# A two-layer decoder trunk: the closing block's seven products reordered with their sums on VectorE, two early weight loads, and one gate step put later

## What is computed

```
even: x + [conv(C*x)*B*silu(g), pooling(u)*silu(g)] @ w_out        after rmsnorm(x) @ w_in
odd:  x + [window attention * silu(g), mLSTM * sigmoid(o) * silu(g)] @ w_out   after rmsnorm(x) @ w_in
out:  rmsnorm(x, final_norm)
```

## Time and profile before

| | |
|---|---|
| median of 3 runs | 1678.21 us (1676.13 to 1678.56) |
| profiled execution, own time | 1675.21 us |
| its span, first to last instruction | 1673.4 us |
| PE busy | 98% of the span |
| granted TensorE clock, mean | 0.996 of full |

### The profile page before, as it was taken

How to read it: one execution, slowest core, us unless ns; L and a number is a source line. 1 busy time by engine, 2 the same in 40 slices (tenths; PEclk the granted TensorE clock), 3 DMA queues, 4 the chain that set the end, 5 groups by cost and what they waited for, 6 DMA issues and landing times.

```text
span 1673.4 us, 20976 instructions
## 1 busy us (share of the span) xinstructions
PE 1643.1 (98%) x7944; PEld 1365.5 (82%) x7944; DVE 869.0 (52%) x1450; ACT 510.2 (30%) x1191; POOL 490.8 (29%) x580
## 2 busy tenths in 40 slices
PE   8999999999999999999999999999999999999996
PEld 8887788888788788888888878888878888888885
DVE  2745335685534662566443475357573236445755
ACT  2000233562200133366310022437441001244732
POOL 8777674547556010000034601000042000100014
PEclk9999999999999999999999999999999999999998
DMA  8887688658898786544679877644498657654456
GB/s 273 312 290 262 221 287 254 207 175 289 302 328 300 260 321 203 168 133 139 239 279 326 290 278 294 199 144 136 143 361 292 196 190 289 241 180 148 138 185 268
DMA packets 180292, 399.18 MB, mean 239 GB/s; under 512 B 34240, under 2 KB 85952, under 8 KB 180192
## 3 DMA queue, kind: packets, MB, share of 16 engines
q1 hardware_dynamic: 157504, 370.20, 64.1%
q10 hardware_dynamic: 22688, 27.64, 5.1%
HBM read 303.35 MB, written 94.44 MB: 238 GB/s over the span
## 4 chain that ended last, share of the span: by engine, by line
PE 89%; DMA 4%; DVE 3%; POOL 2%; issue 1%; ACT 1%; ACTq 0%; POOLq 0%; SPq 0%; DVEq 0%
PE bank L682 14%; PE bank L684 14%; PE bank L683 14%; PE pair_a L682 4%; PE pair_a L684 4%; PE pair_a L683 4%; PE pair_b L682 4%; PE pair_b L684 4%; PE pair_b L683 4%; PE pair_c L682 4%; PE pair_c L684 4%; PE pair_c L683 4%; DMA slot<-split_weights 2%; PE pair_a L1060 2%; PE pair_c L1043 2%
## 5 line engine op out<-in xcount | busy, mean ns | idle before, releaser
L682 PE MATMUL bank<-h_hi,slot 128*128 128x512 f32 (+1 forms) x976 | 381.2, 391 | 2.3 <-DMA slot<-split_weights 1.3
L684 PE MATMUL bank<-h_hi,slot 128*128 128x512 f32 (+1 forms) x976 | 377.4, 387 | 0.0
L683 PE MATMUL bank<-h_lo,slot 128*128 128x512 f32 (+1 forms) x976 | 377.1, 386 | 0.0
L682 PEld LDWEIGHTS bank<-h_hi,slot 128*128 128x128 f32 x976 | 183.8, 188 | 40.5 <-issue 2.7
L684 PEld LDWEIGHTS bank<-h_hi,slot 128*128 128x128 f32 x976 | 183.6, 188 | 37.6
L683 PEld LDWEIGHTS bank<-h_lo,slot 128*128 128x128 f32 x976 | 183.7, 188 | 37.2 <-issue 1.0
L563 POOL TENSOR_TENSOR slot<-stages,slot 128x512 fp32r<-128x512 f32 x132 | 184.9, 1400 | 11.0
L534 POOL TENSOR_TENSOR rs<-sums,eps 128x1 f32<-128x1 f32 x48 | 13.2, 275 | 456.7 <-ACT junk L1197 456.7
L561 POOL TENSOR_SCALAR slot<-stages 128x512 fp32r<-128x512 f32 x132 | 90.6, 686 | 115.1 <-issue 98.3
L624 POOL TENSOR_TENSOR proj<-proj,xin 128x1024 f32<-128x1024 f32 x2 | 4.9, 2444 | 373.6 <-DVE proj L1955 373.6
L682 PE MATMUL pair_a<-h_hi,slot 128*128 128x512 f32 x256 | 101.4, 396 | 1.7 <-DMA slot<-split_weights 1.7
(11 more groups left out here) (349 smaller groups left out, 3428.1 us busy)
## 6 DMA issues: line engine op xcount, KB each, us to landing
slot<-split_weights SPq DMA_DIRECT2D x376, 512.0 KB, 4.4
split_weights<-slot SPq DMA_DIRECT2D x132, 512.0 KB, 4.4
slot<-combined_weights SPq DMA_DIRECT2D x80, 512.0 KB, 5.1
combined_weights<-keys SPq DMA_DIRECT2D x32, 512.0 KB, 5.0
stages<-in_even_w_in SPq DMA_DIRECT2D x48, 256.0 KB, 4.0
stages<-in_odd_w_in SPq DMA_DIRECT2D x36, 256.0 KB, 3.4
stages<-in_even_w_out SPq DMA_DIRECT2D x32, 256.0 KB, 4.0
result<-res ACTq DMA_DIRECT2D x16, 512.0 KB, 7.4
```

Of the source, the lines that this page charges most:

```text
L682: t.matmul(dst, l_hi, r_hi, start=start, stop=False)
L683: t.matmul(dst, l_hi, r_lo, start=False, stop=False)
L684: return t.matmul(dst, l_lo, r_hi, start=False, stop=stop)
```

## The change

1. Only block 3: order Q4, Q1, Q6, Q7, Q5, Q2, Q3 in place of Q2, Q4, Q1, Q5, Q6, Q7, Q3, in other PSUM banks. The four sums and all additions to `res` are DVE's (`last_stage`); POOL keeps the roots. The last tile is scaled and stored in two halves, one by SP and one by ACT. Its tiles 2 and 3 are complete after the fifth product.
2. Loads 0 and 1 of block 1 go to slots 4 and 5, unused in block 0, and are issued before the save of half 128. The ring is turned by four places (`place`).
3. In blocks 1 and 2 the raw loads move from step 0 to step 5, the combined saves from 8 to 35 to 13 to 40.
4. The product `full` and its split move from `gate` of an odd u to `gate` of u + 1, one round later, in all blocks.

```
+ODD_ORDER = ((), (), (Q2, Q4, Q1, Q5, Q6, Q7, Q3), (Q4, Q1, Q6, Q7, Q5, Q2, Q3))
...
+LAST_SUMS = (ODD_SUM2, ODD_SUM3, ODD_SUM1, ODD_SUM4)
...
             def load_half(i):
-                sp.dma_start(slots[i % SLOTS][:, :].bitcast(F32), later[i]).then_inc(s_slot[i % SLOTS], 16)
+                sl = (i + SLOTS0) % SLOTS
+                sp.dma_start(slots[sl][:, :].bitcast(F32), later[i]).then_inc(s_slot[sl], 16)
...
+                if i == HALVES - SLOTS0:
+                    for j in range(SLOTS - SLOTS0):
+                        sp.wait_ge(s_saved[j], 16)
+                        load_half(j)
...
+                sp.wait_ge(s_saved[(SLOTS - SLOTS0 + i) % SLOTS0], 16)
+                sp.wait_ge(s_half, HALVES - SLOTS0 + i + 1)
+                load_half(SLOTS - SLOTS0 + i)
...
-                        if i == 0:
+                        if i == 5:
                             for place in range(4):
                                 load_raw(b - 1, place, 0)
-                        if 8 <= i < 40 and i % 8 < 4:
-                            save_combined(b - 1, 4 * (i // 8 - 1) + i % 8)
+                        if 13 <= i < 41 and (i - 13) % 8 < 4:
+                            save_combined(b - 1, 4 * ((i - 13) // 8) + (i - 13) % 8)
                         if i == 46:
...
+            sp.wait_ge(s_norm, NB * 4)
+            sp.dma_start(out[0][S - 3 * P:S - 2 * P, 0:HALF], res[:, 1, 0:HALF]).then_inc(s_store[1], 16)
...
+                    odd_product(Q4, y_hi[:, 4:8, late], y_lo[:, 4:8, late], 6)
+                    odd_product(Q1, y_hi[:, 0:4, early], y_lo[:, 0:4, early], 2)
+                    summed(ODD_SUM2)
+                    odd_product(Q6, last_hi[ODD_SUM2], last_lo[ODD_SUM2], 4)
+                    pe.wait_ge(s_gated, b * 8 + 8)
+                    summed(ODD_SUM3)
+                    odd_product(Q7, last_hi[ODD_SUM3], last_lo[ODD_SUM3], 0)
+                    summed(ODD_SUM1)
+                    added(Q4)
+                    odd_product(Q5, last_hi[ODD_SUM1], last_lo[ODD_SUM1], 6)
+                    pe.wait_ge(s_odd_copied, m * 2 + 2)
+                    odd_product(Q2, y_hi[:, 4:8, early], y_lo[:, 4:8, early], 2)
+                    summed(ODD_SUM4)
+                    pe.wait_ge(s_odd_twelve, m * 4 + 2)
+                    for t2 in range(2):
+                        for k in range(4):
+                            if t2 == 0:
+                                slot(odd_product_at(b, Q3) - HALVES_TO[b] + k)
+                            last = odd_part(Q3, k, t2, last_hi[ODD_SUM4], last_lo[ODD_SUM4], 4)
+                            if t2 == 1:
+                                last.then_inc(s_half, 1)
+                        if t2 == 0:
+                            last.then_inc(s_three, 1)
...
+                    if 2 <= u <= 8 and u % 2 == 0:
+
+                        j = u // 2 - 1
+                        sync()
                         dve.wait_ge(s_gated, b * 8 + j + 1)
                         full = gate_a if j < 2 and b < SPLIT_OUT else mixed[:, 4 + j, :]
...
+                    dve.wait_ge(s_att_y, b * 4 + 4)
+                    v.tensor_tensor(odd_sum[ODD_SUM1], att_late, mem_late, ALU.add).then_inc(s_odd_sums, 1)
+                    dve.wait_ge(s_odd_sums, m * 4 + 1)
+                    v.tensor_tensor(odd_sum[ODD_SUM2], odd_sum[ODD_SUM1], att_early, ALU.subtract).then_inc(s_odd_sums, 1)
+                    dve.wait_ge(s_odd_sums, m * 4 + 2)
+                    dve.wait_ge(s_yo, b * 8 + 8)
+                    v.tensor_tensor(odd_sum[ODD_SUM3], att_early, att_late, ALU.subtract).then_inc(s_odd_sums, 1)
+                    sum_lo(ODD_SUM2)
+                    dve.wait_ge(s_odd_sums, m * 4 + 3)
+                    v.tensor_tensor(odd_sum[ODD_SUM4], mem_early, odd_sum[ODD_SUM2], ALU.subtract).then_inc(s_odd_sums, 1)
+                    sum_lo(ODD_SUM3)
+                    wait_odd_product(dve, b, Q4)
+                    for tt in range(2):
+                        add(2 + tt, 0, banks[6 + tt])
+                    sum_lo(ODD_SUM1)
+                    for tt in range(2):
+                        dve.wait_ge(s_odd_copied, m * 2 + tt + 1)
+                        add(tt, 0, total[tt])
+                    sum_lo(ODD_SUM4)
+                    wait_odd_product(dve, b, Q6)
+                    for tt in range(2):
+                        dve.wait_ge(s_odd_part, m * 8 + LAST_PARTS[Q1])
+                        v.tensor_tensor(total[tt], total[tt], banks[4 + tt], ALU.add).then_inc(s_odd_twelve, 1)
+                    for tt in range(2):
+                        dve.wait_ge(s_odd_twelve, m * 4 + tt + 1)
+                        add(tt, 1, total[tt])
+                    for tt in range(2):
+                        for n in range(2):
+                            add(2 + tt, n, total[tt])
+                    wait_odd_product(dve, b, Q7)
+                    for tt in range(2):
+                        for n in range(2):
+                            add(2 + tt, n, banks[tt])
+                    wait_odd_product(dve, b, Q5)
+                    for tt in (2, 3, 0, 1):
+                        add(tt, 1, banks[6 + tt % 2])
+                    dve.wait_ge(s_gain, b * 48 + 48)
+                    final_scale(2, 0)
+                    final_scale(3, 1)
+                    wait_odd_product(dve, b, Q2)
+                    for tt in range(2):
+                        add(tt, 0, banks[2 + tt])
+                    dve.wait_ge(s_three, 1)
+                    add(0, 1, banks[4])
+                    wait_odd_product(dve, b, Q3)
+                    add(1, 1, banks[5])
+                    final_scale(0, 2)
+                    dve.wait_ge(s_root, b * 12 + 2 * TT + 4)
+                    for hf in range(2):
+                        final_half(1, hf)
```

More of the change, by code:

```diff
@@ L146, in weights_of @@
         else:
-            found += [odd_weights[p](k) for p in ODD_PRODUCTS for k in range(4)]
+            found += [odd_weights[p](k) for p in ODD_ORDER[b] for k in range(4)]
         assert len(found) == HALVES_OF[b]
@@ L720, in chan_half @@
                 def chan_half(u, h, dst, part):
[L722 removed]
+                    sl = place(at(u, h))
                     for kk in range(4):
@@ L1109, in body @@
                     early, late = slice(0, 2 * P), slice(2 * P, TB)
+                    if closing:
+                        last_products()
+                        return
                     odd_product(Q2, y_hi[:, 4:8, early], y_lo[:, 4:8, early], 4)
@@ L1434, in body @@
                     plain_end(b, sq)
+                elif closing:
+                    last_end(b, sq + 8)
                 else:
-                    seven_end(b, closing, sq + 8)
+                    seven_end(b, sq + 8)
             def load_x(b, tiles):
@@ L1478, in x_squares @@
                 def x_squares(tt):
-                    if not closing:
-                        act.wait_ge(s_x[tt], b * 16 + 32)
-                        for hf in range(2):
-                            next_square(0, xin, tt, hf)
+                    act.wait_ge(s_x[tt], b * 16 + 32)
+                    for hf in range(2):
+                        next_square(0, xin, tt, hf)
                 def sum_hi(i):
@@ L1501, in seven_end @@
                 sum_hi(ODD_SUM4)
-                if not closing:
-                    load_x(b, (2, 3))
+                load_x(b, (2, 3))
                 x_squares(0)
@@ L1513, in seven_end @@
                 x_squares(3)
-                if not closing:
-                    for tt in range(TT):
-                        evacuate(b * 8 + 2 * TT + tt, tt, first_bank=NEXT_BANK[tt])
-                    load_gain(b * 8 + 3 * TT, final_norm)
+                for tt in range(TT):
+                    evacuate(b * 8 + 2 * TT + tt, tt, first_bank=NEXT_BANK[tt])
+                load_gain(b * 8 + 3 * TT, final_norm)
                 for i in range(4):
@@ L1520, in seven_end @@
                     next_square(2, res, 2 + i // 2, i % 2)
-                if closing:
-                    store(b, 2, 0)
-                    store(b, 3, 1)
                 for tt in range(2):
@@ L1527, in seven_end @@
                 for n, tt in enumerate((2, 3, 0, 1)):
-                    if not closing or n >= 2:
-                        store(b, tt, n)
-                if not closing:
-                    act.dma_start(gain[:, :], odd_norm[0].partition_broadcast(P)).then_inc(s_gain, 16)
+                    store(b, tt, n)
+                act.dma_start(gain[:, :], odd_norm[0].partition_broadcast(P)).then_inc(s_gain, 16)
             for b in range(NB):
@@ L1973, in body @@
                     tile2 = b * 8 + 2 * TT
+                    if closing:
+                        last_stage(m)
+                        return
                     def odd_lo_of(i):
```

137 lines of the change are left out of this document (85 added, 52 removed).

## The result

| | before | changed |
|---|---|---|
| median | 1677.64 us (4 runs, 1676.13 to 1678.56) | 1664.28 us (4 runs, 1661.69 to 1667.27) |
| profiled execution, own time | 1675.21 us | 1664.78 us |
| span | 1673.4 us | 1663.0 us |

The ratio is 0.9922, 95% interval 0.9903 to 0.9941. The forecast was 1666.2, in a range of 1663.0 to 1670.5.

What follows compares the result with a forecast made beforehand. PE, busy 98% of the span, bounds the kernel, leaving its waits and both ends to win. Gate 3.2, boundary 3.2 and closing block 5.6 sum to 12.0 us: 1678.2 - 12.0 = 1666.2 us, range 1663 to 1670.5.

Steps and rivals of the forecast that it cites:

- The gate step: Attention of block 0: moving `full` one round later removes PE's two waits for `p_lo`; 3.2 us, bounds 0 and 3.3.
- The boundary: Start of block 1: both PE waits for loads, 1.3 and 1.7 us, go; 3.2 us, bounds 1.5 and 3.3.
- half 6 needed the raw loads moved: Block 1's seventh half: late with 1 MB of raw loads directly ahead on SP's queue; its 1.7 us wait goes.
- The closing block: Block 3's products and end: new order and DVE sums give 6.4 less 0.8, so 5.6 us.
- The tail: From PE's last matmul to the span's end: less work left behind it, span ending 6.4 us sooner, at 1667.0.
- the sign of "under 7": Sign of being right: under 7 us from PE's last matmul to the span's end.
- 0.7 of the stores: Closing products: early stores of tiles 2 and 3 push the last matmuls by 0 to 1.3 us, taken as 0.7.
- 0.1 of Q6: Third closing product: its first low part is ready level with PE's need; 0.1 us of wait, bound 1.5.
- (a): Rival: front waits return in another form, DVE held by POOL or half 6 still late; 1669.4 us, chance 0.17.
- (b): Rival: closing block gives only 3.6 us, Q6 waiting 1.5 and the store costing 1.3; 1668.2 us, chance 0.13.
- (c): Rival: final scales of tiles 2 and 3 don't get ahead of Q3, end gives 0.6 us; 1671.2 us, chance 0.06.
- (d): Rival: combined saves of blocks 1 and 2 reach step 46 and hold up loads; slower, 1688 us, chance 0.03.

Runs made afterwards that it cites:

- early loads alone: Kernel before with only loads 0 and 1 of block 1 put ahead of the save of half 128: 1674.29 us, ratio 0.9976.
- raw loads at once: Changed kernel with the raw loads and combined saves back at steps 0 and 8, run twice: 1667.07 and 1666.76 us.
- later raw loads alone: Kernel before with only raw loads at step 5 and combined saves at 13 to 40 in blocks 1 and 2: 1674.88 us, ratio 0.9982.
- gate alone: Kernel before with only the product `full` and its split one round later: 1674.79 us, ratio 0.9982.
- closing block alone: Kernel before with only block 3's new product order and its sums on DVE: 1672.07 us, ratio 0.9963.
- POOL sums: Changed kernel with block 3's four sums put back on POOL, new order kept: 1668.36 us, ratio 0.9940.
- stores later: Changed kernel with block 3's stores of tiles 2 and 3 issued about 4 us later on ACT, run twice: 1665.16 and 1666.53 us.
- both: Changed kernel with raw loads back at steps 0 and 8 and block 3's stores of tiles 2 and 3 later: 1665.07 us, ratio 0.9917.

## Why the prediction came out

**The gate step, 3.2 us: right**, 3.0 by the ratio of the part alone. What I had named as the risk, a POOL instruction that holds DVE, does happen, though not at `p_lo`: it holds the gate's first factor (line 1987), and PE waits for the second (1988). The result's trace:

```profile
324.20 1.29 POOL L576 TENSOR_TENSOR slot<-stages,slot 128x512 fp32r<-128x512 f32 x1
```

```profile
324.25 1.79 DVE L1987 SCALAR_TENSOR_TENSOR proj<-proj,xin 128x512 f32<-128x512 f32 x1
...
326.69 0.50 PE L695 MATMUL bank<-h_hi,slot 128*128 128x512 f32 x1 [0.64 <-DVE proj L1988]
```

and the same place in the second trace of the changed kernel:

```profile
325.01 0.68 DVE L1987 SCALAR_TENSOR_TENSOR proj<-proj,xin 128x512 f32<-128x512 f32 x1
```

```profile
323.17 1.29 POOL L576 TENSOR_TENSOR slot<-stages,slot 128x512 fp32r<-128x512 f32 x1
...
325.19 0.98 POOL L574 TENSOR_SCALAR slot<-stages 128x512 fp32r<-128x512 f32 x1 [0.72 <-issue]
```

Where POOL starts 0.05 us ahead of DVE, DVE's factor takes 1.79 and PE waits 0.64; where POOL's instruction has ended over 0.5 us before it, the factor takes 0.68 and PE waits for nothing. The wait (0.64 to 0.66) was in four of the nine traces of the changed kernel and its variants; in all four POOL starts 0.05 us ahead, in the five others it has ended 0.54 us or more before.

**The boundary, 3.2 us: the size was right, one reason was not.** Both waits went, and half 6 started 5.80 us earlier (455.00 for 460.80), where the gate and this step together were to give 6.4; the gate's new wait, 0.8 with the 0.16 of a printed one, covers the difference. The step that fell is that half 6 needed the raw loads moved ("It had 1 MB of raw loads directly ahead of it"): the early loads alone removed its wait, and so did every run with the raw loads at once. The later raw loads alone removed it as well: each step is enough, and I had counted on both together. Not each execution of the old code has the full 3.3 us: the gaps at both places come to 3.3, 3.2 and 2.5 in the traces of before, the gate alone and the closing block alone.

**The front and the middle together: right, but not by one pair of traces.** Ahead of the closing block 6.4 us were forecast, and 4.65, 6.0 and 3.6 came in the changed kernel's three traces (first closing product at 1616.73, 1615.37 and 1617.77) against the one of before. More traces have the same code in these stretches. From a matmul near the end of block 0 (at 435.51 in before's trace) to the first closing product they take:

| code of this stretch | us |
|---|---|
| before's: before, gate alone, closing block alone | 1185.9, 1186.7, 1187.2 |
| changed: its three traces, POOL sums, stores later (two) | 1183.6, 1181.7, 1184.4, 1183.4, 1185.1, 1182.5 |
| early loads, raw at once: early loads alone, raw at once (two), both | 1182.8, 1185.9, 1185.6, 1185.7 |
| later raw loads alone | 1184.4 |

The first two rows differ by 3.2 us in the mean, the boundary's 3.2. The matmul itself comes at 436.9 on average in the four traces with the old gate and at 434.0 in the ten with the new one, 2.9 for the gate's 3.2. So most of the 1.6 us that seem missing against before's trace are that trace's own: it was 1.4 and 0.7 us ahead of the mean of its kind. Traces of one code differ by up to 3 us in this stretch and up to 5 in block 0, so these means are good to about 1 us. Three traces of the third row lie over 2 us above the second row's mean and the fourth below it, which is why the worth of the later raw loads stays open. What the forecast did have wrong is that it counted PE's load waits between 470 and 1610 us as fixed. They were 3.2, 4.4 and 4.7 in the first row's traces and 4.6, 3.3 and 5.3 in the changed kernel's, at some ten places where the queue just keeps up.

**The closing block, 5.6 us: right, term by term.** The tail gave 6.2 for 6.4, and ended at 7.0 us, just at the sign of "under 7". The stretch grew by 0.4, 0.6 and 1.4, 0.8 on average, for the 0.7 of the stores and 0.1 of Q6. Q6 was not level, but had 0.7 us to spare: its first low part ended 10.2 us behind the first product's start in place of 10.7, because the four `y_lo` took 0.36 each for 0.43, and the three sums and the low part 1.2 each for 1.25. So Q6's 0.1 did not come. The experiment with the later stores gives the early ones 0.5 us on average; the rest is within the scatter of the traces, and the largest growth, 1.4, lies just over the bound of 1.3. That bound counted one store of 0.5 MB, while the second was issued behind the scale of 1648.80 and met the last loads too, so that 0.7 came out right is in part luck.

**The rivals.** (a) happened in small part: 0.64 us at the gate in some executions, where it would have cost 3.2, and nothing at the boundary. (b) had the stores' bound about right, as the 1.52 us wait shows, and Q6's wrong. (c) did not occur. (d) did not either: SP's longest wait for a combined piece was 8.1 us, as forecast (about 8), the last save of block 1 was issued at 556.70, and at step 46 (568.5) SP waited for PE alone.

```profile
SPq L461 <- POOL keys L630: 72.3, 24, 8.1
```

The sum of 12.0 us compares with 10.4 between the two profiled executions and 13.4 between the medians. That the median fell by more than the trace is scatter of single executions (below); the profiled one of before was 2.4 us under the median above, that of the changed kernel 0.5 over its.

## What to carry to other kernels

At the end of a kernel, count the queue of the engine that finishes the output: here its order, and the engine of four sums ahead of it, were worth 6 us together, while no matmul was saved. When two things stand ahead of a late transfer, take each away alone before saying that both must go. Compare with several traces of the kernel before as well: the one at hand may be a quick one. And an engine pair that blocks each other, as DVE and POOL here, turns a slack of half a microsecond into a coin toss between executions: look at several traces before a wait of 0.6 us is explained.

## What the runs showed of the hardware

I had not expected that the start of one and the same code lasts two different times. Windows of PE (busy us, clock, DMA share, GB/s), first of the changed kernel's second trace, then of the first trace with later stores, whose code is the same up to the last 15 us:

```profile
12.00:16.00 4.00, 2.25 (x14) 0.79 0.53 127
16.00:20.00 4.00, 2.95 (x18) 0.78 0.55 197
20.00:24.00 4.00, 4.00 (x34) 1.00 0.71 240
```

```profile
12.00:16.00 4.00, 2.17 (x17) 1.00 0.54 130
16.00:20.00 4.00, 1.90 (x14) 1.00 0.56 197
20.00:24.00 4.00, 4.00 (x23) 0.57 0.70 233
```

In the first the granted clock is at its lower level (1.2 of 2.4 GHz) for part of the time while PE still waits for data in between, from 12 to 20 us; in the second it falls only after 20 us, where PE is busy without a gap, and 23 matmuls pass in place of 34. From then on the second trace lies 1.4 us behind (the same matmul at 202.69 in place of 201.31). Five of the fourteen traces start in this second way. A second dip comes behind PE's waits of 0.7 and 1.9 us for POOL near 202 to 205 us: from 204 to 214 us the clock is 1.00 in seven traces, 0.83 to 0.85 in five and 0.66 in two. That of the closing block alone has both dips, and its wait for `p_lo` is at 337.31 where before's trace, with the same code so far, has it at 333.14: 4.2 us, 1.4 of them from the first dip. What decides between them no run here shows. It explains a part of the scatter, since single executions of the kernel before lay between 1673.8 and 1684.3 us, and so why the medians of one kernel differ by 1 to 2 us between sets (1664.3, 1664.7 and 1667.0 for the changed one).
